# The router and the first gather of a mixture-of-experts layer: transposes of x itself, scaled router weights, fewer products for the places

## The chip, the cores and the metric

One NeuronCore of one Trainium2 chip runs the whole program. The metric is the device time of one launch in microseconds (us); the median of three runs of the kernel before is 1911.51 us (1910.80 to 1911.77).

## What is computed

Two layers of an encoder trunk on 256 tokens of width 1024, in float32. Each layer has three residual sub-layers: parallel attention mixers, cross-attention into 256 memory tokens, and a channel mixer, which is dense in the first layer and has eight experts, two to a token, in the second. Only the passage from the second layer's cross-attention into its experts is touched here:

```python
x = x + memory_cross_attention(hx, hm, xa_wq[layer], xa_wkv[layer], xa_wo[layer])
hf = rms_norm(x, norm_ffn[layer])            # x * rsqrt(mean(x*x) + eps) * g
logits = hf @ w_router + b_router            # 8 experts
top_val, top_idx = top_k(logits, 2)
gates = one_hot(top_idx) weighed by softmax(top_val)
out = sum_e gates[:, e] * ((silu(hf @ w_g[e]) * (hf @ w_u[e])) @ w_down[e])
x = x + out
```

## The kernel before

**Products in three parts.** Every large product splits both operands into a high part (float32r, copied by ScalarE) and a low part (what is left, subtracted by VectorE) and sums high by high, high by low and low by high in PSUM. Weights come by DMA in units of 1 MB into six slots (`raw`); each unit is two pieces of 128x1024. ScalarE makes a piece's high part `whi` (L546), VectorE its low part `wlo` (L549), in four slots; a slot of `raw` is free for the next transfer when the second `wlo` of its unit is made. With 128 tokens an expert's piece is six products of 512 columns on TensorE (L941, L942 and L954, or L946, L950 and L954 where the rows were just gathered).

**Order.** It is written out by hand: each engine has its own program, and semaphores tie them. Each engine takes its instructions in the order written, so one that waits holds up all that stand behind it.

**End of the cross-attention (layer 1).** The output projection `XO` has two blocks of 512 columns. When a block is summed, VectorE adds it to `x` (L2500) and multiplies by the norm's weight, `h = x * gain` (L2368); ScalarE squares `x` with a running sum (L1623). TensorE transposes `h` (L2026, tile T3: two token halves t by two column halves q, in banks 4 to 7), and ScalarE and VectorE take the high and low parts of the transposes (L1636, L2374). The first column half is done while the second block of `XO` is still being summed. VectorE makes the mean of the squares (L2770, L2773) and GpSimd the power -0.5 (L1430).

**Router.** TensorE holds the router's weights (8 columns) and streams the 256 tokens through them, 24 products (L2287); ScalarE takes the logits out (`logits_T`, L1906), TensorE turns them back to tokens by experts (L2307), VectorE scales them by the tokens' rstd and adds the bias (L1274), finds the two largest (L1284, L1290) and marks them (L1292). TensorE then counts for each token how many earlier ones chose the same expert: five float32 products with a triangle and a block of ones (L2315 to L2319), each of them two instructions. VectorE adds them into the table of places `tab` (L1297) and makes from it the 0/1 matrix `pick` of the first expert (L1153).

**Rows of the first expert.** `h_hi` (ScalarE, L1900) and `h_lo` (VectorE, L1318) are the normed rows in high and low part. The gather is 32 products with `pick` (L888) into banks 2 and 3: all high and low ones of bank 2 first, then those of bank 3. ScalarE and VectorE take `xg_hi` and `xg_lo` from them (L1048, L1159), between the first three weight pieces. After these ScalarE norms `h` in place (L1141), clears the place of the expert before (L1055) and goes on with the pieces; GpSimd finds every expert's rows and scatters them to HBM (L1555 to L1586).

`empty_products` (L912) puts zeros into two banks. `keep_busy` (L867) are transposes of the identity into a bank that nobody reads:

```python
empty_products(pe, "experts")
keep_busy(pe, 1, 8)
pe.wait_ge(choice_ready, at("chosen"))
```

Of the kernel before, what the change touches and what calls it, by code (L numbers as in the profile page):

```python
# [31 lines left out]
P = 128  # L32
# [17 lines left out]
E = 8  # L50
# [253 lines left out]
def trunk(nc, a, out, consts, onehot, known):  # L304
    with ExitStack() as ctx:
# [106 lines left out]
        r_hi = place("r_hi", [P, KD, E], F32R, offset=region + 29 * K1 + 256)  # L412
        r_lo = place("r_lo", [P, KD, E], F32R, offset=region + 29 * K1 + 512)
        r_bias = place("r_bias", [P, E], offset=region + 29 * K1 + 768)
        logits_T = place("logits_T", [E, S], offset=region + 35 * K1)
# [64 lines left out]
        router_low = sem("router_low")  # L480
        rstd_ready = sem("rstd_ready")
# [117 lines left out]
        def cols(l, name):  # L599
            c, n = STAT_COLS[name]  # L600
            return c + 36 * l, n
# [269 lines left out]
        def gather_first(pe, g):  # L871

            pe.wait_ge(expert_step, at(g, "pick", "first"))
            for n_, b in enumerate(ROWS):
# [4 lines left out]
                for low in range(2):  # L879
                    for t in range(NT):  # L880
                        if low:
                            pe.wait_ge(norm_ready, at("h_lo", t))
                        else:
                            pe.wait_ge(high_copied, at("h_hi", t))
                        for i in range(4):
                            k = 4 * n_ + i
                            src = h_lo[:, t] if low else h_hi[t]
                            ins = pe.matmul(bank[b][:, i * P:(i + 1) * P], src[:, k * P:(k + 1) * P], pick[:, t, :],  # L888
                                            start=not low and t == 0 and i == 0, stop=bool(low) and t == NT - 1 and i == 3)
                ins.then_inc(gather_full, mark(gather_full, g, "gather", "first", n_))  # L890
# [257 lines left out]
        def mixer_dve(dve, sp_, g, meanwhile=lambda: None, later=lambda: None):  # L1148
# [7 lines left out]
            def low_gathered(key, which):  # L1156
                for n_, b in enumerate(ROWS):
# [109 lines left out]
        def route(dve):  # L1267


            nothing_yet(dve, "experts")  # L1270
            dve.wait_ge(bank_full[7], at("logits_turned"))
            dve.wait_ge(router_loaded, at("r_b"))
            for t in range(NT):
                dve.scalar_tensor_tensor(rt[:, 0, t], bank[7][:, t * E:(t + 1) * E], rstd(1, "ffn", t), r_bias[:, :],  # L1274
                                         ALU.mult, ALU.add).then_inc(*((dve_freed[7], mark(dve_freed[7], "logits")) if t else
                                                                       (vector_step, mark(vector_step))))
            dve.wait_ge(dve_freed[7], at("logits"))
# [14 lines left out]
            dve.tensor_scalar(rt[:, 5], rt[:, 1], 0.5 * TAKEN, None, ALU.is_lt).then_inc(choice_ready, mark(choice_ready, "chosen"))  # L1292
            dve.wait_ge(choice_ready, at("chosen"))
            step(dve.tensor_scalar(rt[:, 9], rt[:, 5], -4096.0, 4096.0, ALU.mult, ALU.add))
            split_h(dve, 1)
            dve.wait_ge(bank_full[6], at("places"))
            dve.tensor_tensor(tab[:, 0, 0:E, 0:2].rearrange("p e t -> p t e"), bank[6][:, 0:16].rearrange("p (t e) -> p t e", t=NT),  # L1297
                              rt[:, 9], ALU.add).then_inc(vector_step, mark(vector_step, "place table"))
            dve.wait_ge(vector_step, at("place table"))

        def route_gates(dve):
# [6 lines left out]
            step(dve.tensor_tensor(rt[:, 7], rt[:, 6], rt[:, 5], ALU.mult))  # L1308
# [12 lines left out]
        def route_again(dve):  # L1321

            dve.tensor_reduce(rs[:, 10:11], bank[6][:, 16:24], AX.X, ALU.max).then_inc(dve_freed[6], mark(dve_freed[6], "ranks"))
            dve.wait_ge(dve_freed[6], at("ranks"))
# [90 lines left out]
        def _(pool):  # L1415
# [74 lines left out]
            for l in range(DEPTH):  # L1490
# [40 lines left out]
                for t in range(NT):  # L1531
                    normalise(l, "X", t, X_H, smX[:, t])
                power((l, "ffn"), cols(l, "ffn"))
            pool.wait_ge(norm_ready, at(1, "ffn", "h", 1, 1))
# [79 lines left out]
        def _(act):  # L1614
# [102 lines left out]
            for l in range(DEPTH):  # L1717
# [153 lines left out]
                if l:  # L1871
                    act.wait_ge(router_loaded, at("r_b"))
                    act.activation(r_hi[:, :, :], r_raw[:, :, :], ACT.Copy).then_inc(high_copied, mark(high_copied, "r_hi"))
# [16 lines left out]
                to_high(l, "T3", hT_hi, (0,))  # L1890
# [962 lines left out]
```

## Time and profile before

| | |
|---|---|
| median of 3 runs | 1911.51 us |
| the profiled execution's own time | 1911.39 us |
| its span, first to last instruction | 1909.0 us (2.39 us lie around it) |
| TensorE busy | 1881.3 us |
| VectorE busy | 1503.9 us |
| ScalarE busy | 1269.9 us |
| mean granted TensorE clock | 0.997 |
| DMA | 530 MB, mean 278 GB/s |

Busy time says how long an engine had work, not that it set the time. The experts run from 946.8 us of the span to its end, so nearly half of the span follows the passage that the change touches. A granted clock of 1.00 is 2.4 GHz and 0.50 is 1.2 GHz.

### The profile page before, as it was taken

How to read it: one execution, taken by the hardware profiler on the slowest of the kernel's cores; microseconds unless marked ns; L12 is line 12 of the kernel's file. 1: busy time of each engine (PE TensorE's matmuls, PEld its weight loads, DVE VectorE, ACT ScalarE, POOL GpSimd, SP SyncE). 2: the span in 40 equal slices, each digit the busy share in tenths (PEclk: the TensorE clock that was granted, in tenths of full speed). 3: DMA queues.
4: the chain of work that ended last, by engine and by line, in shares of the span. 5: the costliest groups of instructions: out<-in, count | busy, mean ns of one | idle time of the engine just before them, and what ended most of it. 6: DMA issues, size and time to landing. Idle time of an engine off the chain costs nothing.

```text
span 1909.0 us, 27543 instructions
## 1 busy us (share of the span) xinstructions
PE 1881.3 (99%) x9439; PEld 1581.3 (83%) x9439; DVE 1503.9 (79%) x1670; ACT 1269.9 (67%) x1689; POOL 86.6 (5%) x125
## 2 busy tenths in 40 slices
PE   7999999999999999999999999999999999999998
PEld 6887898888888887898788888888888888888886
DVE  4888664645456898665699999999999999999998
ACT  5747543544444747554578888888888788887885
POOL 1020000000000020001220000000000000000000
PEclk9999999999999999999999999999999999999999
DMA  9454653765554453564399999999999999999995
GB/s 341 136 187 133 213 188 132 260 204 194 196 176 139 132 189 123 193 215 137 115 394 404 382 395 352 409 380 371 392 357 407 376 375 384 364 406 377 377 406 199
DMA packets 182590, 530.17 MB, mean 278 GB/s; under 512 B 8896, under 2 KB 18176, under 8 KB 182256
## 3 DMA queue, kind: packets, MB, share of 16 engines
q1 hardware_dynamic: 175136, 503.38, 71.8%
q0 software_dynamic: 4368, 16.69, 2.4%
q10 hardware_dynamic: 3008, 9.07, 1.2%
q8 instruction: 47, 0.77, 0.2%
q14 instruction: 31, 0.25, 0.0%
HBM read 517.56 MB, written 11.56 MB: 277 GB/s over the span
## 4 chain that ended last, share of the span: by engine, by line
PE 91%; DVE 4%; ACT 2%; DMA 1%; issue 1%; POOL 0%; ACTq 0%; DVEq 0%; POOLq 0%; SPq 0%
PE bank L954 16%; PE bank L941 15%; PE bank L942 15%; PE bank L1957 7%; PE bank L1973 7%; PE bank L1965 7%; PE bank L1996 5%; PE bank L731 4%; PE bank L718 4%; PE bank L727 4%; PE bank L2026 2%; PE bank L992 1%; PE bank L2072 1%; DVE wlo L549 1%; DMA raw<-in_moe_w_gu 1%
## 5 line engine op out<-in xcount | busy, mean ns | idle before, releaser
L549 DVE TENSOR_TENSOR wlo<-raw,whi 128x1024 fp32r<-128x1024 f32 (+3 forms) x958 | 1133.8, 1218 | 194.0 <-ACT whi L546 164.0
L546 ACT ACTIVATE whi<-raw 128x1024 fp32r<-128x1024 f32 (+3 forms) x958 | 994.8, 1058 | 279.9 <-PE bank L954 143.8
L941 PE MATMUL bank<-whi,xg_hi 128*128 128x512 f32 x864 | 339.2, 393 | 0.0
L942 PE MATMUL bank<-whi,xg_lo 128*128 128x512 f32 x864 | 336.8, 390 | 0.0
L954 PE MATMUL bank<-wlo,xg_hi 128*128 128x512 f32 x896 | 276.9, 390 | 0.1
L954 PEld LDWEIGHTS bank<-wlo,xg_hi 128*128 128x128 f32 x896 | 168.7, 188 | 36.1 <-DVE wlo L549 0.5
L941 PEld LDWEIGHTS bank<-whi,xg_hi 128*128 128x128 f32 x864 | 162.7, 188 | 33.3 <-ACT whi L546 0.3
L942 PEld LDWEIGHTS bank<-whi,xg_lo 128*128 128x128 f32 x864 | 162.5, 188 | 33.0
L941 PE MATMUL bank<-whi,hidTw_hi 128*128 128x512 f32 x448 | 175.1, 391 | 0.0
L942 PE MATMUL bank<-whi,hidTw_lo 128*128 128x512 f32 x448 | 174.4, 389 | 0.0
L954 PE MATMUL bank<-wlo,hidTw_hi 128*128 128x512 f32 x448 | 138.2, 390 | 0.1
L1957 PE MATMUL bank<-whi,hT_hi 128*128 128x512 f32 (+3 forms) x512 | 133.8, 385 | 1.1 <-ACT hT_hi L1636 1.1
L1973 PE MATMUL bank<-wlo,hT_hi 128*128 128x512 f32 (+3 forms) x512 | 126.7, 372 | 0.2
L1965 PE MATMUL bank<-whi,hT_lo 128*128 128x512 f32 (+3 forms) x512 | 126.9, 372 | 0.0
L1957 PEld LDWEIGHTS bank<-whi,hT_hi 128*128 128x128 f32 x512 | 89.1, 190 | 21.7 <-issue 7.9
L1965 PEld LDWEIGHTS bank<-whi,hT_lo 128*128 128x128 f32 x512 | 92.7, 189 | 15.9
L1973 PEld LDWEIGHTS bank<-wlo,hT_hi 128*128 128x128 f32 x512 | 92.4, 188 | 16.1 <-DVE wlo L549 0.7
L954 PEld LDWEIGHTS bank<-wlo,hidTw_hi 128*128 128x128 f32 x448 | 83.9, 188 | 18.2 <-DVE wlo L549 0.7
L941 PEld LDWEIGHTS bank<-whi,hidTw_hi 128*128 128x128 f32 x448 | 84.1, 188 | 17.3
L942 PEld LDWEIGHTS bank<-whi,hidTw_lo 128*128 128x128 f32 x448 | 84.1, 188 | 17.3
L718 PE MATMUL bank<-whi,hT_hi 128*128 128x512 f32 x224 | 60.6, 392 | 0.0
L731 PE MATMUL bank<-wlo,hT_hi 128*128 128x512 f32 x224 | 60.1, 390 | 0.0
(353 smaller groups left out, 2028.7 us busy)
## 6 DMA issues: line engine op xcount, KB each, us to landing
raw<-in_moe_w_gu SPq DMA_DIRECT2D x224, 1024.0 KB, 7.4
raw<-in_moe_w_down SPq DMA_DIRECT2D x112, 1024.0 KB, 7.5
raw<-in_w_in SPq DMA_DIRECT2D x33, 1024.0 KB, 5.0
raw<-in_ffn_w_gu SPq DMA_DIRECT2D x28, 1024.0 KB, 5.2
raw<-in_xa_wkv SPq DMA_DIRECT2D x16, 1024.0 KB, 5.1
raw<-in_ffn_w_down SPq DMA_DIRECT2D x14, 1024.0 KB, 4.9
raw<-in_w_branch SPq DMA_DIRECT2D x12, 1024.0 KB, 5.1
raw<-in_w_out SPq DMA_DIRECT2D x8, 1024.0 KB, 5.2
```

The lines of the kernel that those rows point to most:

```text
L546: self.eng.activation(whi[:, ps, 0:size], src, ACT.Copy).then_inc(high_ready, mark(high_ready, "high", p))
L549: self.eng.tensor_tensor(wlo[:, ps, 0:size], src, whi[:, ps, 0:size].bitcast(F32), ALU.subtract).then_inc(low_ready, mark(low_ready, "low" ...
L718: pe.matmul(bank[b][:, :], hi, wh, start=st, stop=False)
L727: pe.matmul(bank[b][:, :], lo, wh, start=False, stop=False)
L731: ins = pe.matmul(bank[b][:, :], hi, wl, start=False, stop=en)
L941: pe.matmul(bank[b][:, :], hi[:, k, 0:P], wh, start=first, stop=False)
L942: pe.matmul(bank[b][:, :], lo[:, k, 0:P], wh, start=False, stop=False)
L954: ins = pe.matmul(bank[b][:, :], hi[:, k, 0:P], wl, start=False, stop=last)
L1957: pe.matmul(outs[t], hi[:, k0 + kk, t * P:(t + 1) * P], whi[:, p % PIECE_SLOTS, kk * w_:(kk + 1) * w_], start=k0 + kk == 0, stop=False)
L1965: pe.matmul(outs[t], lo[:, k0 + kk, t * P:(t + 1) * P], whi[:, p % PIECE_SLOTS, kk * w_:(kk + 1) * w_], start=False, stop=False)
L1973: ins = pe.matmul(outs[t], hi[:, k, ts], wl, start=False, stop=k == blk.kt - 1)
L1996: ins = pe.matmul(bank[banks[u]][:, i * S:(i + 1) * S], side[:, p % PIECE_SLOTS, at_:at_ + P], x_of[:, k0 + kk, :], start=side is whi and ...
```

## The change

1. **Transposes of x.** In layer 1 the tile T3 is transposed from `x`, not from `h`; the router's weights are multiplied by the norm's weight beforehand (`r_raw` by `gain_cols`, VectorE, behind the probabilities of the cross-attention). The second half of `h` for both token halves is then made by GpSimd (`late h`). The transpose (t 0, q 1) is taken out by VectorE alone, high part and low part; ScalarE takes (1, 1).
2. **Tokens stationary.** The router's high and low weights lie side by side (16 columns). TensorE holds a 128x128 block of transposed tokens and streams the 16 columns: 32 products, in banks 0 and 1, one bank for each token half. VectorE adds the two halves of the 16 columns with rstd and bias, so `logits_T` and its two transposes are gone.
3. **Places by two products.** The chosen marks and the constants are float32r, and two products (16 and 8 columns) give the places. The counts for the second round are two more products in bank 7.
4. **Rows off the chain.** VectorE makes both `h_lo` behind `pick`, the gates and the ranks behind the first three pieces; the gather does all high parts of both banks first, then the low ones; the first expert's `xg_lo` alternate with the first weight pieces.
5. `keep_busy(pe, 1, 8)` is `keep_busy(pe, 3, 10)`, and `keep_busy(pe, 3, 5)` is new behind the counts. `nothing_yet` (a memset of `scatter`) stands earlier on VectorE; ScalarE makes the float32r constants in an idle place.

```diff
@@ gather_first
-            for n_, b in enumerate(ROWS):
...
-                for low in range(2):
-                    for t in range(NT):
...
+            for low in range(2):
+                for t in range(NT):
...
+                    for n_, b in enumerate(ROWS):
                         for i in range(4):
...
+                        if low and t == NT - 1:
+                            ins.then_inc(gather_full, mark(gather_full, g, "gather", "first", n_))
@@ mixer_dve
             for q in range(3):
                 sp_.one(p0 + q, u0 + q // 2, PIECE * (q % 2), PIECE)
-                if q == 0:
-                    low_gathered(g, "first")
+                if q < 2:
+                    low_gathered(g, "first", (q,))
@@ route
-            dve.wait_ge(bank_full[7], at("logits_turned"))
             for t in range(NT):
...
+                dve.wait_ge(bank_full[t], at("router", t))
+                dve.scalar_tensor_tensor(rt[:, 1, t], bank[t][:, 0:E], rstd(1, "ffn", t), r_bias[:, :], ALU.mult,
+                                         ALU.add).then_inc(vector_step, mark(vector_step))
+                dve.wait_ge(vector_step, tally.total[vector_step])
+                dve.scalar_tensor_tensor(rt[:, 0, t], bank[t][:, E:2 * E], rstd(1, "ffn", t), rt[:, 1, t], ALU.mult,
+                                         ALU.add).then_inc(dve_freed[t], mark(dve_freed[t], "logits", t))
...
-            split_h(dve, 1)
@@ gpsimd
+                if l:
...
+                    for t in range(NT):
+                        pool.wait_ge(dve_freed[lin_bank(l, "XO", 1, t)], at("merge", l, "XO", 1, t))
+                        pool.tensor_tensor(h[:, t, 512:], x[:, t, 512:], gain[0][:, 512:], ALU.mult).then_inc(
+                            late_h, mark(late_h, l, "ffn", "late h", t))
                 power((l, "ffn"), cols(l, "ffn"))
@@ tensor
+                    fill(pe, 0, "dve")
+                    pe.wait_ge(high_copied, at("hi", l, "T3", 0, 0))
+                    router(0, 0, hT_hi)
+                    pe.wait_ge(dve_freed[4], at("lo", l, "T3", 0, 0))
+                    router(0, 0, hT_lo)
+                    turn_x(1, 0)
...
                     empty_products(pe, "experts")
-                    keep_busy(pe, 1, 8)
+                    keep_busy(pe, 3, 10)
...
+                    pe.matmul(bank[6][:, 0:2 * E], earlier, chosen_two[:, :, :], start=True, stop=False)
+                    pe.matmul(bank[6][:, E:2 * E], ones, chosen_two[:, 0], start=False, stop=True).then_inc(
                         bank_full[6], mark(bank_full[6], "places"))
...
+                    keep_busy(pe, 3, 5)
@@ vector
-                add_to_x(l, "XO", 1, 0)
-                times_gain(l, "XO", 1, 0)
-                add_to_x(l, "XO", 1, 1)
-                times_gain(l, "XO", 1, 1)
+                if l:
+                    nothing_yet(dve, "experts")
+                    add_to_x(l, "XO", 1, 0)
+                    add_to_x(l, "XO", 1, 1)
+                    dve.wait_ge(bank_full[5], at(l, "T3", 0, 1))
+                    dve.tensor_copy(hT_hi[:, 4:8, 0:P], heads(bank[5][:, :], 4)).then_inc(
+                        turned_high, mark(turned_high, "hi", l, "T3", 0, 1))
...
+                    mixer_dve(dve, sp_, "experts", split_rows, gates_and_ranks)
```

What stands in the order, at three places. VectorE at the end of the cross-attention, from the second block's sum on, before:

```order
L2500 TENSOR_TENSOR x<-bank,x 128x512
L2368 TENSOR_TENSOR h<-x,gain_99 128x512
L2500 TENSOR_TENSOR x<-bank,x 128x512
L2368 TENSOR_TENSOR h<-x,gain_99 128x512
L2770 TENSOR_TENSOR stats<-stats 128x2
L2773 TENSOR_SCALAR stats<-stats 128x2
L2374 TENSOR_TENSOR hT_lo<-bank,hT_hi 128x4x128 x2
```

and the same place now (L2536 adds to x, L2807 is the new copy of a transpose, L2410 takes low parts):

```order
L1273 MEMSET scatter 128x256
L2536 TENSOR_TENSOR x<-bank,x 128x512 x2
L2807 CAST hT_hi<-bank 128x4x128
L2810 TENSOR_TENSOR hT_lo<-bank,hT_hi 128x4x128
L2821 TENSOR_TENSOR stats<-stats 128x2
L2824 TENSOR_SCALAR stats<-stats 128x2
L2410 TENSOR_TENSOR hT_lo<-bank,hT_hi 128x4x128
```

Two multiplications have left the engine and a copy has come; the second addition follows the first at once. VectorE from the logits to the picks, before:

```order
L1318 SCALAR_TENSOR_TENSOR h_lo<-h,stats,h_hi_122 128x1024
L1265 MEMSET scatter 128x256
L1274 SCALAR_TENSOR_TENSOR rt<-bank,stats,r_bias 128x8 x2
L1284 MAX rt<-rt 128x8 x2
L1286 TENSOR_SCALAR rs<-rt 128x2
L1288 MEMSET rt 128x2x6
L1290 MATCH_REPLACE rt<-rt 128x8 x2
L1292 TENSOR_SCALAR rt<-rt 128x16
L1294 TENSOR_SCALAR rt<-rt 128x16
L1318 SCALAR_TENSOR_TENSOR h_lo<-h,stats,h_hi_123 128x1024
L1297 TENSOR_TENSOR tab<-bank,rt 128x2x8
L1153 TENSOR_SCALAR pick<-cst,tab 128x128 x2
```

and now, from the second token half's logits on:

```order
L1281 SCALAR_TENSOR_TENSOR rt<-bank,stats,r_bias 128x8
L1284 SCALAR_TENSOR_TENSOR rt<-bank,stats,rt 128x8
L1293 MAX rt<-rt 128x8 x2
L1295 TENSOR_SCALAR rs<-rt 128x2
L1297 MEMSET rt 128x2x6
L1299 MATCH_REPLACE rt<-rt 128x8 x2
L1301 TENSOR_SCALAR chosen_two<-rt 128x16
L1303 TENSOR_SCALAR rt<-chosen_two 128x16
L1305 TENSOR_TENSOR tab<-bank,rt 128x2x8
L1160 TENSOR_SCALAR pick<-cst,tab 128x128 x2
L1326 SCALAR_TENSOR_TENSOR h_lo<-h,stats,h_hi_122 128x1024
L1326 SCALAR_TENSOR_TENSOR h_lo<-h,stats,h_hi_123 128x1024
```

Both `h_lo` now stand behind `pick`. TensorE from the last router product to the gather, before:

```order
L2287 MATMUL bank<-hT_lo,r_hi 8x256 x4
L2307 MATMUL bank<-cst,logits_T 128x8 x2
L912 MATMUL bank<-hT_hi,scatter 128x512 x2
L867 MATMUL bank<-cst 128x128 x8
L2315 MATMUL bank<-rt,cst 128x8
L2316 MATMUL bank<-rt,cst 128x8
L2317 MATMUL bank<-rt,cst 128x8
L2318 MATMUL bank<-rt,cst 128x8
L2319 MATMUL bank<-rt,cst 128x8
L888 MATMUL bank<-pick,h_hi_122 128x128 x4
L888 MATMUL bank<-pick,h_hi_123 128x128 x4
L888 MATMUL bank<-pick,h_lo 128x128 x8
```

(the last three rows come twice, once for each bank), and now:

```order
L2317 MATMUL bank<-r_both,hT_lo 128x16 x4
L919 MATMUL bank<-hT_hi,scatter 128x512 x2
L872 MATMUL bank<-cst 128x128 x10
L2349 MATMUL bank<-chosen_two,before_ones 128x16
L2350 MATMUL bank<-chosen_two,before_ones 128x8
L2353 MATMUL bank<-chosen_two,before_ones 128x8
L2354 MATMUL bank<-chosen_two,before_ones 128x8
L872 MATMUL bank<-cst 128x128 x5
L894 MATMUL bank<-pick,h_hi_122 128x128 x8
L894 MATMUL bank<-pick,h_hi_123 128x128 x8
L894 MATMUL bank<-pick,h_lo 128x128 x16
```

Only the first two of the four new products stand ahead of the places, and no high part of the gather waits for a low one.

## Rows read from the trace of the kernel before

**Rows 1.** The page: busy time by engine, and the chain's shares.
```profile
PE 1881.3 (99%) x9439; PEld 1581.3 (83%) x9439; DVE 1503.9 (79%) x1670; ACT 1269.9 (67%) x1689; POOL 86.6 (5%) x125
PE 91%; DVE 4%; ACT 2%; DMA 1%; issue 1%; POOL 0%; ACTq 0%; DVEq 0%; POOLq 0%; SPq 0%
```
**Rows 2.** Busy time in stretches: length, engines (instructions), clock, DMA share, GB/s.
```profile
960.00:1000.00 40.00, 39.81 (x178) 32.26 (x177) 35.58 (x34) 30.37 (x35) 6.31 (x4) 1.00 1.02 407
1300.00:1400.00 100.00, 100.00 (x453) 82.99 (x452) 92.43 (x84) 81.79 (x85) 0.00 (x0) 1.00 1.01 388
```
**Rows 3.** Waits, 952 to 1897 us: total us, times, longest.
```profile
ACT whi L546 <- DMA raw<-in_moe_w_gu: 8.8, 11, 2.1
...
PEld bank L954 <- DVE wlo L549: 1.2, 3, 0.5
```
**Rows 4.** Timeline, end of the cross-attention: start, us, engine, what [idle before].
```profile
931.86 0.69 DVE L2500 TENSOR_TENSOR x<-bank,x 128x512 f32<-128x512 f32 x1 [3.69 <-PE bank L1973]
...
933.33 0.66 PE L2026 MATMUL bank<-cst,h 128*128 128x128 f32 x4
...
933.91 0.63 ACT L1623 ACTIVATE merged<-x 128x512 f32<-128x512 f32 x1 [0.54 <-DVE x L2500]
...
935.27 0.71 POOL L1430 TENSOR_TENSOR stats<-stats 128x2 f32<-128x2 f32 x1 [38.65 <-DVE stats L2773]
...
936.01 1.15 ACT L1900 ACTIVATE h_hi<-h,stats 128x1024 fp32r<-128x1024 f32 x1
```
**Rows 5.** Timeline, VectorE, 893 to 912 us: a copy of a bank.
```profile
898.97 0.69 DVE L2459 COPY pTX<-bank 128x512 f32<-128x512 f32 x1 [1.25 <-PE bank L2026]
```
**Rows 6.** GpSimd's multiplications of 128x1024, ns min/median/max.
```profile
L1453 POOL TENSOR_TENSOR smX<-smX,sstats x4: 1891/2290/2696, 312.2 to 893.9; 128x1024 f32<-128x1024 f32 x4
```
**Rows 7.** Timeline, from the logits to the gather.
```profile
938.75 0.23 DVE L1274 SCALAR_TENSOR_TENSOR rt<-bank,stats,r_bias 128x8 f32<-128x8 f32 x2
...
939.92 0.17 DVE L1292 TENSOR_SCALAR rt<-rt 128x16 f32<-128x16 f32 x1
...
940.29 0.30 PEld L2315 LDWEIGHTS bank<-rt,cst 128*128 128x128 f32 x2
...
940.34 1.29 DVE L1318 SCALAR_TENSOR_TENSOR h_lo<-h,stats,h_hi 128x1024 fp32r<-128x1024 f32 x1
...
941.21 0.37 PE L2319 MATMUL bank<-rt,cst 128*128 128x8 f32 x2
...
941.61 0.19 DVE L1297 TENSOR_TENSOR tab<-bank,rt 128x16 f32<-128x16 f32 x1
941.83 0.48 DVE L1153 TENSOR_SCALAR pick<-cst,tab 128x128 fp32r<-128x128 f32 x2
...
942.37 1.11 PE L888 MATMUL bank<-pick,h_hi 128*128 128x128 f32 x8 [0.80 <-DVE pick L1153]
```
**Rows 8.** Timeline, from the gather to the fourth weight piece.
```profile
945.10 1.89 PE L888 MATMUL bank<-pick,h_lo 128*128 128x128 f32 x8
...
947.03 0.60 ACT L1048 ACTIVATE xg_hi<-bank 128x512 fp32r<-128x512 f32 x1 [2.02 <-PE bank L888]
...
951.51 1.06 ACT L546 ACTIVATE whi<-raw 128x1024 fp32r<-128x1024 f32 x1
...
952.60 10.33 DVE L549 TENSOR_TENSOR wlo<-raw,whi 128x1024 fp32r<-128x1024 f32 x9 [1.54 <-ACT whi L546]
```
**Rows 9.** The chain in order of time: products of the second and fourth piece.
```profile
949.66 0.43 PE bank L941
...
954.46 0.45 PE bank L954 x2
```
**Rows 10.** Stretches of 1 us: TensorE's granted clock is the number behind POOL's.
```profile
944.00:945.00 1.00, 1.00 (x12) 1.00 (x11) 0.23 (x1) 0.59 (x1) 0.83 (x3) 1.00 0.00 0
945.00:946.00 1.00, 1.00 (x8) 1.00 (x7) 0.69 (x1) 0.01 (x1) 0.69 (x4) 0.55 0.00 0
...
951.00:952.00 1.00, 1.00 (x4) 0.74 (x4) 0.06 (x1) 1.00 (x3) 0.69 (x4) 0.53 0.71 193
```

More of the change, by code:

```diff
@@ L873, in gather_first @@
             pe.wait_ge(expert_step, at(g, "pick", "first"))
-            for n_, b in enumerate(ROWS):
+            for b in ROWS:
                 if tally.total[b, "act"]:
@@ L1890, in _ @@
                 to_high(l, "T3", hT_hi, (0,))
+                if l:
+                    act.wait_ge(consts_loaded, at("consts"))
+                    act.activation(before_ones[:, :], cst[:, C_TRI:C_TRI + 2 * P], ACT.Copy).then_inc(
+                        before_ready, mark(before_ready, "before and ones"))
                 act.wait_ge(piece_used, at("lin", l, "XO", 1, 1))
@@ L1904, in _ @@
                     high_of_h(0)
-                    act.wait_ge(bank_full[0], at("router"))
-                    act.activation(logits_T[:, :], bank[0][0:E, 0:S], ACT.Copy).then_inc(
-                        act_freed[0], mark(act_freed[0], "logits_out"))
                     high_of_h(1)
@@ L2283, in _ @@
                 linear(l, "XO", 1, hT_hi, hT_lo, first=2)
                 if l:
-                    def router(hi, lo, k, st, en):
-                        return pe.matmul(bank[0][0:E, 0:S], hi[:, k], lo[:, k], start=st, stop=en)
-                    pe.wait_ge(router_low, at("r_lo"))
-                    fill(pe, 0, "act")
-                    for q in range(2):
-                        if q:
-                            turn_all(l, "T3", h, norm_ready, lambda q, t: (l, "ffn", "h", q, t), (1,))
-                        for t in range(NT):
-                            pe.wait_ge(high_copied, at("hi", l, "T3", t, q))
-                        for k in range(4 * q, 4 * q + 4):
-                            router(r_hi, hT_hi, k, k == 0, False)
-                            router(r_lo, hT_hi, k, False, False)
-                        for t in range(NT):
-                            pe.wait_ge(dve_freed[4 + 2 * t + q], at("lo", l, "T3", t, q))
-                        for k in range(4 * q, 4 * q + 4):
-                            ins = router(r_hi, hT_lo, k, False, k == KD - 1)
@@ L2303, in _, with router @@
-                    ins.then_inc(bank_full[0], mark(bank_full[0], "router"))
-                    pe.wait_ge(act_freed[0], at("logits_out"))
-                    fill(pe, 7, "dve")
-                    for t in range(NT):
-                        ins = pe.transpose(bank[7][:, t * E:(t + 1) * E], logits_T[:, t * P:(t + 1) * P], ident[0:E, 0:E])
-                    ins.then_inc(bank_full[7], mark(bank_full[7], "logits_turned"))
+                    def router(t, q, of):
+                        for k in range(4 * q, 4 * q + 4):
+                            ins = pe.matmul(bank[t][:, 0:2 * E], of[:, k, t * P:(t + 1) * P], r_both[:, k, :],
+                                            start=of is hT_hi and k == 0, stop=of is hT_lo and k == KD - 1)
+                        return ins
@@ new lines, in _ @@
+                    pe.wait_ge(router_low, at("r_lo"))
+                    fill(pe, 0, "dve")
[4 more added lines that the diff above has]
+                    turn_x(1, 0)
+                    fill(pe, 1, "dve")
+                    pe.wait_ge(high_copied, at("hi", l, "T3", 1, 0))
+                    router(1, 0, hT_hi)
@@ new lines, in _ @@
+                    pe.matmul(bank[6][:, 0:2 * E], earlier, chosen_two[:, :, :], start=True, stop=False)
+                    pe.matmul(bank[6][:, E:2 * E], ones, chosen_two[:, 0], start=False, stop=True).then_inc(
+                        bank_full[6], mark(bank_full[6], "places"))
+                    fill(pe, 7, "dve")
+                    pe.matmul(bank[7][:, 0:E], ones, chosen_two[:, 0], start=True, stop=False)
+                    pe.matmul(bank[7][:, 0:E], ones, chosen_two[:, 1], start=False, stop=True).then_inc(
+                        bank_full[7], mark(bank_full[7], "counts"))
```

117 lines of the change are left out of this document (78 added, 39 removed).

## The prediction

> **What bounds the kernel now.** The page first: TensorE is busy for 1881 of 1909 us and the chain of waits lies on it for 91% [rows 1]. The table of stretches then tells which stages are full: 100 us in the middle of the experts hold 100.00 us of TensorE at full clock [rows 2]. The list of waits over all experts leaves TensorE next to nothing: its longest entry is 1.2 us, for `wlo` [rows 3]. So whatever brings TensorE to the first expert's pieces earlier moves all that follows with it, unless the transfers can't follow: from 960 to 1000 us they run at a share of 1.02, TensorE already idles 0.19 us there [rows 2], and ScalarE waited 8.8 us for them in all [rows 3].
>
> The passage itself is what TensorE does not fill. In the timeline the second block's sum reaches VectorE at 931.86 [rows 4], the gather starts at 942.37 behind `pick` [rows 7], and the fourth weight piece ends at 954.46 + 0.45 = 954.91, from where the chain has no gap [rows 9]. I compare that instant before and after. Between them lie two costs: the chain of small steps, and a clock that falls from 1.00 to 0.50 within the second that begins at 945 and comes back at the end of the one that begins at 951 [rows 10]. The shares 0.55 and 0.53 put the fall at 945.1 and the return at 951.94, so 6.8 us at 1.2 GHz.
>
> **The change, step by step.** *End of the cross-attention.* The two additions now follow each other, 931.86 + 2 x 0.69 = 933.24. The transposes of (0, 1) wait only for the first; ahead of them stand 8 router products at about 0.11 us (nearest row: eight 128-column products in 1.11 with the last one's 0.28 drain [rows 7]; with 16 columns the load of the weights sets it), from 931.9 to 932.8. Transposes 0.66 [rows 4], VectorE's copy from 933.47, 0.69 as the nearest copy of a bank [rows 5], and the subtraction 0.69: 934.87. The squares (0.63 + 0.19 each) are done by 934.2 and hide. The mean's two small operations end at 935.23, some 0.1 later than now. GpSimd's two late multiplications are half of 1.89 to 2.70, so 0.95 to 1.35 each [rows 6], from 932.6 to 934.5 or 935.3: hidden at best, 0.1 late at worst; I take hidden. The power ends at 936.1 (now 935.98, [rows 4]): **nothing gained by here**, and `h_hi` starts 0.1 later.
>
> *Logits and choice.* The last router products follow VectorE's last low part (935.94) and are through at 936.55. Four small operations of 0.2 us each, two before and two after that, give the logits at 937.0, where they stand at 938.75 + 0.23 now [rows 7]: **2.0 us earlier**, since `h_lo`, `logits_T` and its transposes no longer lie ahead. From there to the marks nothing changes (938.13 for 940.09).
>
> *Places.* Now 1.5 us pass from the marks (940.09) to `tab` (941.61): ten loads and products, and `h_lo` of 1.29 on VectorE beside them [rows 7]. Two products with one load each cost a fifth of the ten (five pairs, first load at 940.29, last pair at 941.21, so 0.23 apart), 0.25, and 0.3 of latency: `tab` at 938.7, `pick` done at 939.4, gather at 939.43. **2.9 us earlier** than 942.37. The 10 fillers end at 938.05, the counts and 5 fillers at 939.3: neither holds up what is behind it.
>
> *Gather and rows.* 16 high products at 0.11 reach 941.2. VectorE makes both `h_lo` behind `pick`: 939.4 + 2 x 1.28 = 941.95, so the last eight products wait to 942.1, bank 2 is complete at 942.7 and bank 3 at 943.2. ScalarE: exponentials, table load and two `whi` end at 942.3, so it takes `xg_hi` at 942.74 and 943.24, where the second starts at 947.03 now. From there to the fourth `whi` its work is unchanged, 951.51 - 947.03 = 4.48 [rows 8]: 947.7 to 948.8. VectorE makes `xg_lo` by 944.1, `wlo` of the third piece by 947.0, then gates (0.9) and ranks (0.5), which lay before them; 948.4, still ahead of the fourth `whi`. Its fourth `wlo` starts at 948.8 instead of 952.60 [rows 8]: **3.8 us earlier**.
>
> *TensorE at 2.4 GHz.* First piece from 943.4, held by `xg_lo` to 944.1, done 945.1; six products of 0.227 each [rows 9] make 1.365 for a piece: 947.85 after the third. Then it idles for `whi` to 948.85 and ends the fourth at 950.5: 4.4 earlier. But units come free only 3.8 earlier with VectorE's fourth `wlo`, and the transfers have no more than 0.19 us to give [rows 2]. With a full clock the sum is therefore 3.8, **1911.39 - 3.8 = 1907.6** for the profiled execution. It stands 0.12 under the median of the three runs, which changes nothing.
>
> *The clock.* What price it takes the trace shows only for the old order: the second piece's products took 0.43 each [rows 9], 2.56 for a piece in place of 1.365, and eight gather products 1.89 in place of 1.11 [rows 8]. TensorE was busy when it fell; what went before were 8 us of short work with gaps. The new order has as many gaps and shorter products (16 columns for 256). I see nothing that would keep the clock up and expect a fall of about the same 6.8 us near the old place. Falling at 945.1 again: pieces end at 945.1, 947.7, 950.2, the fourth at 952.4, a gain of 2.5. Falling at the end of the gather, some 3 us earlier: it comes back at about 948.5 and half of it lies under the idle time before the fourth `whi`: 3.2. Some 3 us later it hits pieces that wait for nothing: 1.6. I take 2.7: 1911.39 - 2.7 = **1908.7**.
>
> **The rivals.** *Full clock* (0.32). The fillers and the shorter gaps keep 2.4 GHz, or the fall lies wholly under waits; 1907.6 by the sum above, 1907.0 if the transfers follow by 4.4. For it: the clock was 1.00 through all the gaps from 932 to 945 [rows 10]; against: it did fall in the end, with fillers there too.
>
> *The clock falls before the gather* (0.16). If the 16-column products and the fillers count for little, 1.2 GHz begins at 938 to 939. 32 gather products at 0.22 (eight in 1.89, [rows 8]) take 7.1 instead of 3.6, to 946.6; ScalarE's fourth `whi` comes at 951.2 to 952.2, the fourth piece ends between 953.9 and 954.6: gain 0.3 to 1.0, **1910.7**. The Trainium skill, "TensorE: Matmul & The Clock Gate", Part 4 on transposes, says that transposes don't count as busy time for the clock in the way that products do. By that rule the 15 fillers are no cover, and this rival would be the forecast. The trace neither bears it out nor refutes it: 8 fillers ended at 940.3, and the fall came at 945.1, in the gather.
>
> *Slower than before* (0.05). The same early fall, but lasting. Counting pieces, the new order stands level with the old if 1.2 GHz covers the gather and ends at 952.3; each us beyond costs 1 - 1.365/2.56 = 0.47. An end at 955.7 gives 1.6 more: **1913.0**; 0.2% slower would need 960.5. Against it: in the old order the clock was back within 5.2 us of the first piece's start.
>
> *The gain doesn't arrive* (0.05). The chain before the logits is longer than reckoned: GpSimd's late multiplications, slowed beside VectorE, hold the power back. At twice their upper price, 2.7 each, the power would come at 938.0 in place of 935.3 and eat 2.7 us: about **1911.3**.
>
> **How the numbers follow.** 0.2% is 3.8 us, about what a measurement of this kernel can tell from no change, so under 1907.7 counts as faster and over 1915.3 as slower. Chances: forecast 0.42, full clock 0.32, early fall 0.16, slower 0.05, no gain 0.05. The range is 1906.9 to 1911.3: below, the full clock with transfers that follow; above, the early fall; outside it are the slower case and little more. Of the full clock's 0.32 two thirds fall under 1907.7, and 0.03 of the forecast's edge: faster 0.24; of the slower case most stays within 0.2%: slower 0.04; within 0.2% 0.72.
>
> **What would show each step.** In the new profile: GpSimd's power ending near 936.1; `pick` at 938.9 and the first gather product at 939.4; the second `xg_hi` of ScalarE at 943.2; the fourth `wlo` of VectorE starting at 948.8; TensorE idle before the fourth `whi` if the clock is full and busy throughout if it fell; the place of 0.50 in the granted clock. Wrong would be: a power ending after 936.5 (GpSimd mis-sized), a gather that waits for `h_hi`, a stretch from 960 to 1000 us with over 1 us of idle TensorE (transfers bind harder than I took), or a clock that is slow before 939.

## The result: slower, by a wait that stands 33 us behind the change

| | before | changed |
|---|---|---|
| median (runs) | 1911.15 (4) | 1921.47 (4: 1919.12 to 1923.63) |
| ratio, 95% interval | | 1.0055 [1.0042, 1.0067] |
| profiled execution, its span | 1911.39, 1909.0 | 1919.64, 1917.6 |
| mean granted clock of that execution | | 0.996 |

The page of the changed kernel, to be read against [rows 1]:

```profile
PE 1880.4 (98%) x9446; PEld 1582.5 (83%) x9446; DVE 1504.3 (78%) x1672; ACT 1270.2 (66%) x1688; POOL 99.6 (5%) x127
PE 90%; DVE 3%; ACT 2%; POOL 2%; DMA 1%; issue 1%; ACTq 0%; DVEq 0%; POOLq 0%
```

TensorE is busy for as long as before within 0.9 us, but GpSimd is busy 13.0 us longer than the 86.6 of before with two instructions more, and it now has 2% of the chain, where it had none. So the page by itself points at GpSimd.

**The passage that was forecast.** Timeline of the changed kernel: start, us, engine, what, and the idle time before it.

```profile
932.77 2.51 POOL L1546 TENSOR_TENSOR h<-x,gain 128x512 f32<-128x512 f32 x2 [36.08 <-DVE x L2536]
...
935.58 0.70 POOL L1439 TENSOR_TENSOR stats<-stats 128x2 f32<-128x2 f32 x1 [0.30 <-DVE stats L2824]
...
939.02 0.19 DVE L1305 TENSOR_TENSOR tab<-bank,rt 128x16 f32<-128x16 f32 x1 [0.36 <-PE bank L2350]
939.25 0.48 DVE L1160 TENSOR_SCALAR pick<-cst,tab 128x128 fp32r<-128x128 f32 x2
...
939.78 2.00 PE L894 MATMUL bank<-pick,h_hi 128*128 128x128 f32 x16
...
943.16 1.09 ACT L1055 ACTIVATE xg_hi<-bank 128x512 fp32r<-128x512 f32 x2 [0.86 <-PE bank L894]
...
947.27 0.17 DVE L1316 TENSOR_TENSOR rt<-rt,chosen_two 128x16 f32<-128x16 f32 x1
...
948.12 1.07 ACT L551 ACTIVATE whi<-raw 128x1024 fp32r<-128x1024 f32 x1
949.22 6.98 DVE L554 TENSOR_TENSOR wlo<-raw,whi 128x1024 fp32r<-128x1024 f32 x6 [0.74 <-ACT whi L551]
...
950.50 0.73 PE L961 MATMUL bank<-wlo,xg_hi 128*128 128x512 f32 x2
```

The gather starts 2.6 us earlier (939.78 for 942.37). The fourth piece ends at about 950.50 + 0.45 = 950.95 (two products 0.23 apart, as in [rows 9]) for 954.91: 4.0 us earlier. Up to here the change does what it says.

**Where it was lost.** Waits of the changed kernel, 955 to 1905 us (total us, times, longest), against [rows 3]:

```profile
ACT whi L551 <- DMA expert_inputs<-h,put_at: 13.6, 1, 13.6
...
PE bank L948 <- ACT whi L551: 11.4, 1, 11.4
```

One wait each, and neither stood in the list of before. Timeline of ScalarE and of TensorE there:

```profile
980.40 1.09 ACT L1101 ACTIVATE hidw<-bank 128x512 f32<-128x512 f32 x2
994.54 0.37 ACTq L1076 DMA_DIRECT2D xrows<-expert_inputs  x1
995.10 3.90 ACT L551 ACTIVATE whi<-raw 128x1024 fp32r<-128x1024 f32 x4 [13.60 <-DMA expert_inputs<-h,put_at]
```

```profile
984.16 0.61 PE L961 MATMUL bank<-wlo,xg_hi 128*128 128x512 f32 x2
996.21 0.80 PE L948 MATMUL bank<-whi,xg_hi 128*128 128x512 f32 x1 [11.43 <-ACT whi L551]
```

ScalarE's queue holds, in the middle of the first expert, `load_rows`: the load of the next expert's rows, behind a wait for GpSimd's four scatters of rows. ScalarE reaches it at 981.5 and stands until 994.5, the `whi` queued behind it stand too, and TensorE runs dry. Stretches of the changed kernel (columns as in [rows 2]) show what this takes with it:

```profile
980.00:985.00 5.00, 4.78 (x22) 3.62 (x20) 2.00 (x3) 1.50 (x4) 3.36 (x4) 1.00 1.01 406
985.00:990.00 5.00, 0.00 (x0) 0.00 (x0) 0.00 (x0) 0.00 (x0) 0.00 (x0) 0.93 1.03 415
990.00:995.00 5.00, 0.00 (x0) 0.00 (x0) 0.00 (x0) 0.00 (x0) 0.00 (x0) 0.50 0.30 122
995.00:1000.00 5.00, 3.79 (x10) 3.03 (x11) 3.81 (x4) 4.72 (x5) 0.00 (x0) 0.55 0.42 116
```

The compute engines stand still. The transfers go on for a while (share 1.03, then 0.30), but without a new `wlo` no slot of `raw` comes free for them. The granted clock falls to 0.50, 1.2 GHz, so that work taken up at 996.21 runs at half speed for 3.3 us more. The account against the profiled execution of before: 4.0 gained, 11.4 idle, half of 3.3 at the slow clock: 11.4 + 1.7 - 4.0 = 9.1 us slower; measured 1919.64 - 1911.39 = 8.25.

The 0.8 between them can be placed by two marks, TensorE's first two groups of transposes of `hidw` in the first expert (L992 before, L999 now). The first starts at 978.29 for 981.95, 3.7 us earlier, 0.3 less than at the fourth piece; the second at 1025.09 for 1016.39, 8.7 us later. So 12.4 us were lost between them where 11.4 + 1.7 = 13.1 were counted: the kernel before itself lost 0.7 there, with two waits of its weight loads for `wlo`, 0.5 us each, that the changed kernel doesn't have there. From there the distance stays 8.7 to the last products (1906.41 for 1897.71); 0.1 of it comes back behind them, and 0.35 outside the span (2.04 us lie around it now, 2.39 before).

**Why the scatters came late.** GpSimd, changed kernel:

```profile
948.21 0.18 POOL L1571 MEMSET chosen<- 128x96 f32 x1 [11.03 <-DVE tab L1321]
...
949.09 0.27 POOL L1574 TENSOR_SCALAR chosen<-tab 128x16 f32<-128x16 f32 x1
949.44 1.08 POOL L1575 TENSOR_TENSOR chosen<-chosen 128x16 f32<-128x16 f32 x1
950.60 1.07 POOL L1576 TENSOR_TENSOR chosen<-chosen 128x16 f32<-128x16 f32 x1
...
967.37 7.22 POOL L1593 TENSOR_TENSOR terms<-terms 128x16 f32<-128x16 f32 x9
...
976.91 1.22 POOL L1596 COPY row_gate<-terms 128x4 f32<-128x4 f32 x1
979.08 1.35 POOL L1602 DMA_INDIRECT expert_inputs<-h,put_at  x1 [0.95 <-POOL row_gate L1596]
...
983.30 0.97 POOL L1602 DMA_INDIRECT expert_inputs<-h,put_at  x1 [0.30 <-issue]
```

and GpSimd, kernel before:

```profile
943.18 0.18 POOL L1555 MEMSET chosen<- 128x96 f32 x1 [6.30 <-DVE tab L1313]
...
944.81 0.22 POOL L1559 TENSOR_TENSOR chosen<-chosen 128x16 f32<-128x16 f32 x1
...
948.46 1.11 POOL L1571 TENSOR_TENSOR terms<-terms,chosen 128x16 f32<-128x16 f32 x1
...
958.51 1.07 POOL L1580 COPY row_gate<-terms 128x4 f32<-128x4 f32 x1
960.51 1.14 POOL L1586 DMA_INDIRECT expert_inputs<-h,put_at  x1 [0.94 <-POOL row_gate L1580]
...
965.77 1.97 POOL L1586 DMA_INDIRECT expert_inputs<-h,put_at  x1 [0.30 <-issue]
```

GpSimd searches for each expert's rows with 31 small operations behind the gates' table (`tab`, written by `route_gates` on VectorE). The change put the gates behind the low parts of the first three pieces. So the search starts 5.0 us later, and takes 978.13 - 948.21 = 29.9 us where it took 16.4: the same operation of 128x16 takes 1.08 us when it starts within one of VectorE's `wlo` subtractions, whose two inputs lie in SBUF (the core's working memory), and 0.22 where VectorE is idle. Of the 29 operations of the search that read SBUF, 9 started within such a subtraction before and 23 do now. The others found VectorE idle (one of them in a step of 128x1) or in a subtraction with one input in PSUM (`bank`), which doesn't slow them either. Here are four additions of the changed kernel beside two such subtractions, all four in 1.06 us:

```profile
970.08 1.06 POOL L1593 TENSOR_TENSOR terms<-terms 128x16 f32<-128x16 f32 x4
...
969.84 1.28 DVE L1215 TENSOR_TENSOR hidw<-hidw,bank 128x512 f32<-128x512 f32 x2
```

That accounts for the 13.6. The last scatter was issued at 965.77 before and landed 11.0 us later (the longest of the four, 8.4 to 11.0), so the rows were there at 976.7, and the load was issued at 983.82: 7.0 us in hand. Now the search starts 5.0 later and takes 13.5 longer, but the four issues behind it are 1.0 quicker, so the last scatter goes out 17.5 later (983.30) and lands 11.1 later, at 994.4. ScalarE comes to the load 2.3 earlier (981.5): 17.5 + 0.1 + 2.3 - 7.0 = 12.9 us until the rows are there, and 0.7 for the load's own issue.

### The profile page after: what moved, and what is told of

Its sections match the earlier page's. It is cut to its first block, busy times and chain, and to the rows that moved or that the text cites. A ratio compares the mean times of both kernels' runs of the same rounds, so it can differ in the third digit from the quotient of the medians.

```text
span 1917.6 us, 27569 instructions
## 1 busy us (share of the span) xinstructions
PE 1880.4 (98%) x9446; PEld 1582.5 (83%) x9446; DVE 1504.3 (78%) x1672; ACT 1270.2 (66%) x1688; POOL 99.6 (5%) x127
## 4 chain that ended last, share of the span: by engine, by line
PE 90%; DVE 3%; ACT 2%; POOL 2%; DMA 1%; issue 1%; ACTq 0%; DVEq 0%; POOLq 0%
PE bank L961 15%; PE bank L948 15%; PE bank L949 15%; PE bank L1978 7%; PE bank L1994 7%; PE bank L1986 7%; PE bank L2017 5%; PE bank L723 4%; PE bank L736 4%; PE bank L732 4%; PE bank L2047 2%; PE bank L999 1%; PE bank L2093 1%; DVE wlo L554 1%; PE bank L2287 1%
## 5 line engine op out<-in xcount | busy, mean ns | idle before, releaser
L948 PEld LDWEIGHTS bank<-whi,xg_hi 128*128 128x128 f32 x864 | 162.9, 189 | 45.7 <-ACT whi L551 13.1
```

What stands on the lines that cost most here:

```text
L948: pe.matmul(bank[b][:, :], hi[:, k, 0:P], wh, start=first, stop=False)
```

## The experiments

The theory after this reading: the gates' place starts GpSimd's search late and beside VectorE's two-input subtractions, and ScalarE's queued wait for its rows turns that into idle TensorE. Rivals: something else in the change (the gather's new order, the clock, the transfers) starved the first expert; or the search was late only because of GpSimd's new late multiplications.

**e1: gates back ahead of the low parts of the tokens.** In the changed kernel:

```diff
 def split_rows():
+    route_gates(dve)
     for t in range(NT):
         split_h(dve, t)
 def gates_and_ranks():
-    route_gates(dve)
     route_again(dve)
```

> The changed kernel with the gates taken ahead of the two h_lo again (five small VectorE operations moved back), ranks left late. Theory (late rows): the changed kernel lost because GpSimd's search for rows starts at 948.2 us instead of 943.2 and then runs wholly beside VectorE's low parts at 1.1 us an operation instead of 0.22, so that ScalarE, which has the load of the next rows in its queue at 981.5 us, waits 13.6 us for the scatters. With the gates early the search starts near 940.3; 39 operations at 0.2 to 1.1 us end between 958 and 970, the scatters land between 976 and 986: no wait at all to a wait of 4 us. Total 1907.5 without a wait, up to 1910 with it. Rival (transfers): the weights and scatters together are what is late, whatever the start; then it stays near 1919 to 1923. Rival (chain): the head of the chain got no faster; then 1911 at best.

Measured: median 1907.84 (1906.65 to 1910.11, 11 runs), ratio to before 0.9985 [0.9976, 0.9994]. (The search has 31 operations, not the 39 of this expectation and of e3's.) Waits, and one stretch, of e1:

```profile
ACT whi L551 <- DMA expert_inputs<-h,put_at: 1.7, 1, 1.7
```

```profile
960.00:1000.00 40.00, 40.00 (x181) 32.98 (x180) 36.69 (x36) 31.33 (x34) 9.12 (x9) 1.00 1.02 404
```

GpSimd starts at 940.62 and issues the scatters from 966.01 on; the last one lands at 983.05 and ScalarE's load follows 0.02 us behind it. Five instructions in another place take 13.6 us off the median; everything else of the change stays in. The rows still come 1.7 us late for ScalarE, but TensorE has work for that long.

**e2: the load one step later.** The gates stay late; only ScalarE's load moves:

```diff
-                    if j == 1 and not last_trip:
+                    if j == 2 and not last_trip:
                         load_rows(key, expert)
```

> The changed kernel with ScalarE's load of the next expert's rows one block of 1024 columns later (about 33 us later in each expert; its reader on TensorE comes another 30 us behind). Late rows: the scatters are still late (landing near 994 us) but nobody waits; no idle stretch of TensorE near 985 us, no 1.2 GHz there, and the 4.0 us won by the fourth piece stay: 1907.4. Rival (transfers): ScalarE waits for weights instead and 8 us or more of idle TensorE stay between 980 and 1000: 1915 or more. Rival (the idle stretch is only half of the loss, the slow clock behind it the other): no difference in this run; both go.

Measured: 1909.18 (1908.8 to 1910.26, 11), ratio 0.9993 [0.9984, 1.0002]. GpSimd is as late as ever (search from 950.59, scatters from 981.46 to 985.70), and the list of waits has no entry for the rows. A stretch of e2 in which the changed kernel stood still:

```profile
985.00:990.00 5.00, 5.00 (x24) 4.14 (x23) 4.87 (x5) 4.04 (x5) 1.62 (x2) 1.00 1.02 411
```

So a late search by itself makes no idle time; the price is made by the wait in ScalarE's queue. The median is 1.8 us above the 1907.4 that I had expected and 1.3 above e1's. In the profile of e2 the clock is at 1.2 GHz from about 935.3 to 942.1, ahead of the late gates, and the fourth `wlo` starts at 951.60 for 949.74 in e1, whose profile has no such stretch. Of e2's 11 runs none has a mean clock above 0.997, of e1's six have. Why the two kernels differ in this is open.

**e3: the kernel before, with nothing of the change but the late gates.**

```diff
-mixer_dve(dve, sp_, "experts", lambda: route_gates(dve), lambda: route_again(dve))
+mixer_dve(dve, sp_, "experts", lambda: None, lambda: (route_gates(dve), route_again(dve)))
```

> The kernel before with one thing changed: the gates are computed behind the first three pieces, beside the ranks. Late rows: the table is ready near 951.4 instead of 943.1, GpSimd's 39 operations take 28 to 30 us, the scatters are issued at 981 to 986 and land near 996; ScalarE reaches its load at 987 and waits 9 us, of which TensorE sees some 7: slower by 8 to 12 us with the slow clock, 1919 to 1923. Rival (transfers or the new chain are to blame, not the place of the gates): 1911, no change.

Measured: 1923.1 (1922.85 to 1924.68, 5), ratio 1.0065 [1.0051, 1.0079]. Its waits:

```profile
POOL chosen L1555 <- DVE tab L1313: 15.3, 1, 15.3
ACT whi L546 <- DMA expert_inputs<-h,put_at: 13.6, 1, 13.6
...
PE bank L941 <- ACT whi L546: 11.4, 1, 11.4
```

The same 13.6 and 11.4 as in the changed kernel, and more than the 9 and 7 that I had expected. The gates' place alone makes the whole loss, and the rest of the change isn't needed for it; that ends both rivals.

**e5: VectorE's subtractions made into fills.** The low part of the experts' weights, from the fourth piece on, is left out of the result and zeros are written in its place. What the search meets is changed, not the place of the gates:

```diff
+    if p >= segments[1][1] + 3:
+        self.eng.memset(wlo[:, ps, 0:size].bitcast(F32), 0.0).then_inc(low_ready, mark(low_ready, "low", p))
+        return
     self.eng.tensor_tensor(
```

> The changed kernel with the low parts of the experts' weights, from the fourth piece on, written as zeros by a memset on VectorE instead of a subtraction of two tensors in SBUF; the low part of those weights is left out of the result. Everything else, the late gates and the place of the load included, is as in the changed kernel. Late rows through contention: GpSimd's search starts at 948.2 as before, but its small operations take 0.2 to 0.3 us instead of 1.1, the scatters land before 981 us and ScalarE does not wait: 1907.5. Rival (GpSimd is slow there for another reason, ScalarE's or the transfers' work): operations stay at 1.1 us, the wait of some 13 us stays, 1919 to 1923.

Measured: 1909.07 (1906.24 to 1910.92, 11), ratio 0.9987 [0.9978, 0.9996]. GpSimd in e5:

```profile
950.53 0.18 POOL L1574 MEMSET chosen<- 128x96 f32 x1 [13.28 <-DVE tab L1324]
...
951.76 0.22 POOL L1578 TENSOR_TENSOR chosen<-chosen 128x16 f32<-128x16 f32 x1
...
956.30 2.51 POOL L1596 TENSOR_TENSOR terms<-terms 128x16 f32<-128x16 f32 x9
...
960.57 1.11 POOL L1605 DMA_INDIRECT expert_inputs<-h,put_at  x1 [0.94 <-POOL row_gate L1599]
```

The search starts 2.3 us later than in the changed kernel and is done in 9.1 us instead of 29.9; nine operations take 2.51 for 7.22. Beside fills, which read nothing, every small operation is back at 0.2 to 0.3, and the list of waits has no entry for the rows. A fill takes 0.91 us for a subtraction's 1.22, so VectorE is also less busy here; the operations that start within a fill take 0.19 to 0.27 all the same. The Trainium skill, "SBUF — State Buffer", section "Who interferes with whom", says that a VectorE instruction with two SBUF inputs contends with a GpSimd instruction that reads SBUF, and that the order of issue decides which of the two blocks. The traces agree on the first: in the changed kernel GpSimd's operations start 1.15 us apart from 949.44 to 958.69, one to each subtraction (these start 1.15 apart too), and each ends some 0.1 us behind the end of the subtraction in which it started. Of GpSimd's holding up VectorE they show nothing: the subtractions take 1.22 us there as elsewhere. The forecast should have weighed this rule for the search as well, and didn't.

**e7: the control for e2,** the later load in the kernel before:

> The kernel before with the load of the rows a block later and nothing else. There the scatters had landed before ScalarE came to the load, so nothing waits and nothing changes: 1911.0, ratio 1.000 within 0.001. If the later load alone were worth something, as a rival to the head of the chain for the 1.7 us that the changed kernel with the later load is ahead, it shows here as 1909 to 1910.

Measured: 1910.51 (1910.03 to 1911.58, 11), ratio 0.9998 [0.9989, 1.0007]. The later load is worth nothing where nothing waits for rows.

**e6: both repairs together.**

> The changed kernel with both remedies: gates ahead of the two h_lo and the load of the rows a block later. The run with the gates early still had a wait of 1.7 us on ScalarE without idle time on TensorE, so the second remedy should bring nothing beyond it: 1907.8, same as the gates alone, with the search starting at 940.6. If that wait did cost, up to 1 us less: 1906.8.

Measured: 1908.8 (1906.63 to 1909.82, 11), ratio 0.9986 [0.9977, 0.9995]. Not better than e1: either repair takes away all of TensorE's idle time, and the 1.7 us that ScalarE still waits in e1 cost nothing that shows here. The 11 runs fall into two groups, 1906.6 to 1907.0 and 1908.7 to 1909.8, which leads to the clock.

**e4: e2 without the fillers** (both `keep_busy` calls ahead of the gather taken out), **and e8: e6 with products of 512 columns for fillers,** 5 and 2 of them for 10 and 5 transposes (the first of the two places):

```diff
-                    keep_busy(pe, 3, 10)
+                    pe.wait_ge(dve_freed[3], now(dve_freed[3], tally.total[3, "dve"]))
+                    for _ in range(5):
+                        pe.matmul(bank[3][:, :], hT_hi[:, 0, 0:P], hT_hi[:, 0:2, :], start=True, stop=True)
```

> As the run with the later load, and without the fifteen filler transposes (ten ahead of the places, five behind the counts). If the fillers are what kept the granted clock at 1.00 through the passage in the changed kernel, it falls to 0.50 somewhere between 938 and 952 us and part of the gain goes: 1908.5 to 1911. If the denser chain is enough, or transposes count for nothing, the clock stays at 1.00 and the time is that of the later load, 1907.4.

> As with both remedies, but the fifteen filler transposes replaced by seven products of 512 columns into the same unread bank, of about the same length (five ahead of the places, two behind the counts). If transposes count for less than products for the granted clock, this holds 2.4 GHz more firmly through the passage and the slower ones among the runs (1909 to 1910 with the gates early) go: median 1907.0, no run above 1908. If they count alike, the same spread and median as with both remedies, 1907.8.

Measured: e4 1910.03 (1908.77 to 1912.1, 11), ratio 0.9997 [0.9988, 1.0006]; e8 1908.01 (1906.79 to 1912.59, 11), ratio 0.9991 [0.9982, 1.0]. Neither differs from its partner in time by more than the intervals. What e8 was to show if products hold the clock better, no run above 1908, didn't come: six of 11 are above it, two of them at 1912.4 and 1912.6. The mean clock of the single runs says a little more. Without fillers all 11 runs have 0.994 or 0.995; e2, with them, has 0.997 in 10 of 11. With transposes 4 of 11 runs of e6 have 0.998 or 0.999, with long products 5 of 11 of e8. The profiles fit: 1.2 GHz for 6.8 us in e2's, for 13.7 in e4's. So the fillers shorten the slow stretch, and between transposes and products these runs show no difference.

**e9 and e10: a place between.** e1's gates hold the tokens' low parts back by 0.8 us, and in the changed kernel VectorE waits 0.54 us a little later, behind the first piece's low part. e9 puts the gates between the two; e10 is e1 again, measured together with e9.

```diff
 def split_rows():
     for t in range(NT):
         split_h(dve, t)
+    route_gates(dve)
```

> The changed kernel with the gates behind both low parts of the tokens and ahead of the first piece's low part. In e1 the gates stood ahead of those low parts and held them back by 0.8 us; here they fill a gap: in the changed kernel VectorE waits 0.54 us for the second xg_hi before its first xg_lo. Theory (the search's start decides, the gates otherwise cost only what they hold back on VectorE): search from about 943.1, its small operations beside VectorE's work mostly at 1.08 us from 949 on, scatters issued by 969 to 973, rows landed by 983; ScalarE's wait for them 2 to 5 us at most and TensorE idle under 3 us; the fourth piece 0.2 to 0.3 us earlier than in e1. Time 1907 to 1910. Rival (any start of the search behind the tokens' low parts is as bad as behind the third piece, since all of it then lies beside the subtractions): a wait of 8 us or more on ScalarE, time 1914 or more.

> The same kernel as e1, for a comparison on one chip with e9. Expected as there: 1907 to 1910, search from 940.6, no idle time of TensorE for the rows. If e9 is level with it within 0.5 us, either place of the gates will do.

Measured: e9 1911.72 (1908.52 to 1914.32, 11), ratio 1.0005 [0.9996, 1.0014]; e10 1907.37 (1906.73 to 1910.44, 11), ratio 0.9986 [0.9977, 0.9996]. I had expected e9 at 1907 to 1910, and that is a miss. GpSimd and the waits in e9:

```profile
942.61 0.18 POOL L1571 MEMSET chosen<- 128x96 f32 x1 [6.58 <-DVE tab L1321]
...
955.06 10.70 POOL L1593 TENSOR_TENSOR terms<-terms 128x16 f32<-128x16 f32 x9
...
975.54 1.97 POOL L1602 DMA_INDIRECT expert_inputs<-h,put_at  x1 [0.30 <-issue]
```

```profile
ACT whi L551 <- DMA expert_inputs<-h,put_at: 5.5, 1, 5.5
...
PE bank L948 <- ACT whi L551: 4.1, 2, 3.4
```

The search starts 2.0 us later than in e1, and its last scatter is out at 977.5 for 971.3 there. Of these 6.2 us the start makes 2.0, the search 1.7 (26.1 us for 24.4, though it meets hardly more subtractions, 19 for 18) and the scatters 2.6: three issues take 1.91 to 1.97 for 0.96 to 1.05. Why the issues are slower here is open. The rows come 5.5 us late, TensorE idles 3.4. Place by place the wait is 1.7 (e1, search from 940.6), 5.5 (e9, 942.6), 13.6 (the change, 948.2): between the kernel that wins 3 us and the one that loses 10 lie 7.6 us in the start of one search. The version to keep is e1, faster than before in both of its measurements (0.9985 and 0.9986, upper ends 0.9994 and 0.9996) and 13 to 14 us faster than the change as it came.

## Why the prediction was wrong, step by step

- **The step that failed** is the one on VectorE's `wlo`: "then gates (0.9) and ranks (0.5), which lay before them; 948.4, still ahead of the fourth `whi`". For VectorE it is right: they end at 948.5 in the trace. But it is the end of VectorE's part only. The gates were a moved step, costed on VectorE alone, and the question who waits for them was not asked. GpSimd's search waits for them, ScalarE waits for what it scatters, and TensorE for ScalarE: 11.4 us idle and 1.7 at the slow clock, against a forecast of 0.
- **What the trace of before showed already:** `POOL chosen <- DVE tab`, a wait of GpSimd for just this table, then 16.4 us of search with both prices in it, 0.22 and 1.11, the scatters, and 7.0 us in hand at the load. From these rows the search could be bounded at 31 us (27 operations, 1.15 apart), so 14.6 longer. With the prediction's own times (gates done at 947.0 + 0.9 = 947.9 for 943.1, ScalarE 3.8 earlier at the load) the wait on ScalarE could be bounded at 4.8 + 14.6 + 3.8 - 7.0 = 16.2; it was 13.6.
- **The end of the cross-attention** came near: power done at 936.28 (forecast 936.1), GpSimd's late multiplications 1.26 each (bounds 0.95 to 1.35). **Logits and choice:** 937.36 for 937.0, marks 938.45 for 938.13. **Places:** `tab` starts at 939.02 for 938.7; `pick` is done at 939.73 for 939.4. **Gather:** 939.78 for 939.43. All are 0.3 late, and most of that is the power's 0.2.
- **Rows and pieces:** fourth `whi` at 948.12 (947.7 to 948.8), fourth `wlo` at 949.22 (948.8), fourth piece's end 950.95 (950.5), so 4.0 earlier for 4.4.
- **The sum at full clock,** 1907.6, is what the repaired kernel does: in the 22 runs of e1 and e10, the 12 with a mean clock of 0.998 or 0.999 took 1906.65 to 1907.88. Part of this is luck. At the first group of transposes of `hidw` e1's profile is 3.1 us ahead of before (978.82 for 981.95), not 3.8; at the second it is 3.8 ahead (1012.56 for 1016.39). The 0.7 between them are the waits for `wlo` that the kernel before had there. The prediction had allowed 0.19 for this stretch: it counted TensorE's idle time alone, and waits that the list books on the weight load [rows 3] don't show in that.
- **The clock.** The forecast took 1.1 us off the gain for a fall. In the changed kernel's profiled execution the clock was 1.00 through the passage until the idle time at 985. But other executions have the fall: the four runs of e1 and e10 with a mean clock of 0.995 took 1909.68 to 1910.44. The forecast's 1908.7 lies between these two kinds of run.
- **The rivals.** "Full clock" was right for the passage and in half of the repaired runs. "The clock falls before the gather" does occur: stretches of e2 show it at 935 to 942,

```profile
935.00:940.00 5.00, 5.00 (x24) 4.70 (x24) 3.23 (x17) 3.49 (x6) 1.73 (x3) 0.53 0.28 104
940.00:945.00 5.00, 5.00 (x38) 5.00 (x37) 3.85 (x6) 2.60 (x4) 0.00 (x0) 0.79 0.00 1
```

  and costs less than I had put on it: e2's profiled execution took 1908.82, not 1910.7. "The gain doesn't arrive" had GpSimd slowed beside VectorE, the right mechanism, at two long multiplications that hide, and not at the search, which doesn't. The slower case was hung on the clock alone, with a price of 1 to 2 us; no rival let a wait on another engine's queue cost ten. The range, up to 1911.3, allowed for no new wait behind the fourth piece.
- **The test I had named,** more than 1 us of idle TensorE from 960 to 1000, did find it: 28.57 busy of 40. I had written the transfers down as its cause.

## What to carry to other kernels

When a step is moved off the critical chain, follow its result to every reader on every engine, and on from there until the chain is met again; compute how much time each of these has in hand, and take the prices of the neighbourhood into which the work moves, not of the one that it leaves. A wait in the queue of an engine that feeds the bound is a deadline for all that stands before it: here it sat 33 us behind the moved step, and moving the wait one step later, or the step back, was worth 12 to 14 us. Short GpSimd operations that read SBUF were cheap here only while VectorE wasn't reading two operands from it.

## What the runs showed of the chip

- A GpSimd operation of 128x16 that reads SBUF took 0.22 us beside an idle VectorE, one that only fills, or one whose subtraction of 128x512 has an input in PSUM. It took 1.01 to 1.29 us, mostly 1.08, where it started within a subtraction of 128x1024 with both inputs in SBUF (23 operations of the changed kernel). A fill on GpSimd, which reads nothing, took 0.18 us within such a subtraction (943.18 in the kernel before). The subtraction itself paid nothing that could be seen: 1.22 us.
- The issue of one indirect scatter on GpSimd took 0.96 to 1.97 us; the same four instructions, in different kernels. The last of the four landed 10.6 to 13.3 us after its issue, and ScalarE's load followed within 0.03 us of that wherever it had been waiting (the changed kernel, e1, e3, e9).
- The granted clock of the same program differs between executions. The repaired kernel has its passage at 1.00 in e1's profiled execution; in that of e10, the same program, these stretches show 1.2 GHz from about 938 to 951:

```profile
935.00:940.00 5.00, 4.82 (x31) 4.42 (x32) 3.79 (x22) 3.85 (x5) 1.39 (x3) 0.78 0.28 105
940.00:945.00 5.00, 5.00 (x26) 5.00 (x24) 4.00 (x7) 2.10 (x3) 3.84 (x8) 0.50 0.00 0
945.00:950.00 5.00, 5.00 (x18) 4.36 (x18) 2.92 (x4) 3.30 (x5) 3.96 (x14) 0.50 0.00 0
```

  The profiled times are 1907.16 and 1910.05, so some 3 us of what single runs of this kernel differ by go with the clock. In e10 GpSimd's search took 15.8 us for e1's 24.4. The start times say why: 8 of the search's operations in e10 start within a subtraction of two SBUF inputs, 18 in e1, and ten times the 0.86 between 1.08 and 0.22 is the difference of 8.6. In e10 VectorE had waited 3.0 us for the first `xg_hi` (0.24 in e1) and ScalarE 4.3 for TensorE's gather ahead of it (1.4). That the slow clock makes these waits is my reading and wasn't tested by itself.
